# Hybrid attention layer: key and query projection moved two units ahead, MoBA gating interleaved with attention

## The reference, cut to what matters

```python
o_a = _merge_heads(_dilated_mixture(qa, ka, va)) * jax.nn.silu(ga)
o_b = _merge_heads(_moba_attention(qb, kb, vb)) * jax.nn.silu(gb)
...
k_mean = kb.astype(jnp.float32).mean(axis=3)
gate = jnp.einsum('bhsd,bhnd->bhsn', q.astype(jnp.float32), k_mean)
gate = jnp.where(past, gate, NEG_INF)
_, sel = lax.top_k(gate, topk)
```

## Time and profile before

| what | us |
|---|---|
| median of 2 runs | 2077.74 (2073.84 to 2081.64) |
| the profiled execution | 2058.25 |
| its span, on its slowest core, core 1 | 2056.6 |
| spans of the 8 cores | 2040.9 to 2056.6 |
| busy: PE, DVE, ACT, POOL | 1395.1, 1116.9, 989.0, 374.3 |

### The profile page before, as it was taken

The page is one execution under the profiler, slowest core; times in us unless marked ns, Lnnn a source line. Parts: engine busy times, 40 slices in busy tenths (PEclk is TensorE's granted clock), DMA queues, the critical chain, the costliest instruction groups (busy, mean ns, idle before and its releaser), DMA issues.

```text
span 2056.6 us, 24938 instructions; the slowest of 8 cores (2040.9 to 2056.6 us)
## 1 busy us (share of the span) xinstructions
PE 1395.1 (68%) x7432; PEld 596.8 (29%) x7432; DVE 1116.9 (54%) x2347; ACT 989.0 (48%) x1601; POOL 374.3 (18%) x269
## 2 busy tenths in 40 slices
PE   1558888878676666757551888887858576766762
PEld 0114333323242433323110423333314242422220
DVE  0005667675746464554462566766683646464475
ACT  0035657566455464644221575765636465555300
POOL 1011111111101010102454111111111110111276
PEclk9769989898979797978775898989888888896876
DMA  9362020202201000022656202022020200010233
GB/s 304 106 118 28 1 21 1 21 3 20 22 1 16 6 1 1 3 39 64 171 184 114 21 1 22 1 21 22 1 22 1 21 1 1 1 29 13 71 124 133
DMA packets 91868, 90.07 MB, mean 44 GB/s; under 512 B 69246, under 2 KB 73600, under 8 KB 91484
## 3 DMA queue, kind: packets, MB, share of 16 engines
q1 hardware_dynamic: 21020, 67.51, 10.4%
q0 software_dynamic: 70720, 20.98, 10.2%
HBM read 92.67 MB, written 16.78 MB: 53 GB/s over the span
## 4 chain that ended last, share of the span: by engine, by line
PE 45%; DVE 17%; ACT 12%; issue 11%; DMA 7%; POOL 4%; SPq 2%; DVEq 0%; ACTq 0%; POOLq 0%
PE st L578 12%; PE ot L623 11%; PE st L291 7%; PE pr L521 6%; ACT pbuf L585 5%; DMA QT<-x 4%; PE pp L536 3%; ACT pbuf L590 3%; PE pp L203 2%; POOL QT L794 2%; POOL KT L792 2%; DVE tmpf L318 2%; DVE kms L380 2%; DMA modp<-bada 2%; DVE pbuf L602 1%
## 5 line engine op out<-in xcount | busy, mean ns | idle before, releaser
L585 ACT ACTIVATE pbuf<-st 128x1024 bf16<-128x1024 f32 x384 | 381.3, 1024 | 175.6 <-PE st L578 173.6
L578 PE MATMUL st<-QT,KT 64*128 64x512 bf16 (+7 forms) x1280 | 377.7, 379 | 106.0 <-ACT pbuf L585 43.9
L623 PE MATMUL ot<-pbuf,Vt 128*128 128x512 bf16 (+3 forms) x1280 | 366.3, 370 | 68.7 <-DVE pbuf L602 50.5
L643 POOL TENSOR_TENSOR catT<-rcp,catT 64x512 bf16<-64x512 f32 x128 | 147.6, 1153 | 1139.2 <-DVE rcp L639 733.7
L602 DVE TENSOR_TENSOR pbuf<-pbuf,maskA_sb 128x512 bf16<-128x512 bf16 (+3 forms) x640 | 258.9, 451 | 174.9 <-ACT pbuf L585 125.8
L590 ACT ACTIVATE pbuf<-st 128x512 bf16<-128x512 f32 (+3 forms) x512 | 192.7, 441 | 322.0 <-PE st L578 320.0
L291 PE MATMUL st<-hT,wball 128*128 128x512 bf16 x1088 | 257.4, 383 | 68.6 <-DMA wball<-w_in 68.6
L639 DVE TENSOR_TENSOR rcp<-ot,rcp 64x512 f32<-64x512 f32 x128 | 88.1, 689 | 240.0 <-ACT rcp L637 239.7
L758 PE MATMUL st<-wball,catT 128*128 128x512 bf16 x512 | 145.7, 451 | 83.5 <-DVE KT L769 76.1
L623 PEld LDWEIGHTS ot<-pbuf,Vt 128*128 128x128 bf16 x1280 | 97.3, 100 | 281.1 <-issue 236.8
L578 PEld LDWEIGHTS st<-QT,KT 64*128 64x128 bf16 (+1 forms) x1280 | 91.6, 99 | 286.9 <-issue 257.2
(11 more groups left out here) (94 smaller groups left out, 1343.5 us busy)
## 6 DMA issues: line engine op xcount, KB each, us to landing
wball<-w_in POOLq DMA_DIRECT2D x64, 256.0 KB, 7.4
QT<-x SPq DMA_DIRECT2D x32, 512.0 KB, 4.9
y<-QT SPq DMA_DIRECT2D x32, 512.0 KB, 2.9
catT<-w_ada SPq DMA_DIRECT2D x2, 4096.0 KB, 25.3
xs<-xT SPq DMA_DIRECT2D x32, 256.0 KB, 5.8
hT<-w_ada SPq DMA_DIRECT2D x1, 4096.0 KB, 22.8
QT<-xT SPq DMA_DIRECT2D x8, 512.0 KB, 14.0
KT<-xT SPq DMA_DIRECT2D x8, 512.0 KB, 15.3
```

The costliest lines, as they stand in the source:

```text
L578: ev = op("pe", (lambda o, l, r: (lambda e: e.matmul(o, l, r, start=True, stop=True)))(stp[sti][:, jj * 512 + c0:(jj + 1) * 512], ksl[rows ...
L585: ev_e = op("act", (lambda pb_, sv, c: (lambda e: e.activation(pb_[:, :, c:512], sv[:, :, c:512], AF.Exp, scale=0.125)))(pbuf[pbi], stv, c ...
L623: ev = op("pe", (lambda o, l, r, f: (lambda e: e.matmul(o, l, r, start=f, stop=False, skip_group_check=True)))(otp[oi][:, c0:512], Vt[qi][ ...
L643: e3 = op("pool", (lambda n_, orow_, tk: (lambda e: e.tensor_tensor(catT[orow_, u, tk], n_[orow_, :], catT[orow_, u, tk], op=ALU.mult)))(r ...
```

## The change

`proj_unit` loses its gating. The loop calls it for unit u+2 after the attention of unit u, so two units are projected ahead; unit 1 is projected before the loop. The SiLU step in it works on the gate of unit u+1 (`silu_u`), and unit 7's gate, for which no projection is left, gets its SiLU alone (`silu_only`). The gating becomes a generator of 28 steps, `gating_gen`, that a new `merge3` lays beside the attention of the unit before: one attention step, one filler chunk, one gating step. It uses bank `pp` alone, and the filler uses bank `pr` alone.

```diff
@@ proj_unit
-            if u + 2 < 8:
-                load_weights(b, u + 2)
-            rope_done = S_.last("dve", "pool", "act")
...
+            state["qk_done"] = S_.last("dve", "pool", "act") + extra_ready
+            state["kmean_ev"] = kmean_ev[0]
@@ gating
-            def gating_both():
-                qts, kts = QT[qi], KT[qi]
-                gbanks = [pr, pp]
...
+        def gating_gen(b, u):
...
+                    ev = op("pe", (lambda q, h: (lambda e: e.matmul(
+                        pp[:, h * 256 + q * 16:h * 256 + (q + 1) * 16], qts[h][0:64, q * 128:(q + 1) * 128], kmhl2[0:64, h, :],
+                        start=True, stop=True)))(q16, hh),
...
+                for piece in range(4):
+                    bank = pp
+                    fkey = "pp_free"
...
+                            waits=([e11] + list(state[fkey]) if i4 == 0 else ()),
+                            sig=(True if i4 == 3 else None))
+                    yield
+                    e12 = op("dve", (lambda pc, h, bk: (lambda e: e.tensor_copy(
+                        qts[h][64:72, pc * 512:(pc + 1) * 512], bk[64:72, :])))(piece, hh, bank),
+                        waits=[ev], sig=True)
+                    state[fkey] = [e12]
+                    yield
@@ vg_filler
-            banks = [[pr[:, :], "pr_free"], [pp[:, :], "pp_free"]]
+            banks = [[pr[:, :], "pr_free"]]
...
-                bank, fkey = banks[n % 2]
+                bank, fkey = banks[0]
@@ main loop
             run(proj_unit(b, 0, hT_ready, full=True))
+            load_weights(b, 2)
+            run(proj_unit(b, 1, hT_ready, full=False, silu_u=None))
             for u in range(8):
-                ready = list(state["unit_ready"])
...
+                ready = S_.last("dve", "pool", "act") + e8_all
+                if u < 7:
+                    gg = gating_gen(b, u + 1) if u + 1 >= 4 else None
+                    merge3(att_unit(b, u, ready), vg_filler(b, u + 1), gg)
+                    state["wb_free"][(u + 1) % 2] = list(state["fill_last_pe"])
+                    if u + 3 < 8:
+                        load_weights(b, u + 3)
+                    if u + 2 < 8:
+                        run(proj_unit(b, u + 2, hT_ready, full=False, silu_u=u + 1))
+                        e8_all += e8_events()
+                    else:
...
+                        silu_only(b, u + 1)
+                else:
                     run(att_unit(b, u, ready))
-                    merge(att_unit(b, u, ready), vg_filler(b, u + 1), 1.0)
-                    run(proj_unit(b, u + 1, hT_ready, full=False))
```

More of the change, by code:

```diff
@@ L412, in proj_unit @@
                 for tt in range(4):
-                    steps += [lambda tt=tt: qk_step(1, tt), lambda tt=tt: silu_step(tt)]
+                    steps += [lambda tt=tt: qk_step(1, tt)]
+                    if silu_u is not None:
+                        steps += [lambda tt=tt: silu_step(tt)]
+                if silu_u is None:
+                    steps += [flush_step]
+                nk = len(steps)
                 steps += [lambda tt=tt: qk_step(0, tt) for tt in range(4)]
                 if is_b:
-                    steps.insert(9, flush_step)
-                    steps.insert(10, kmean_step)
+                    steps.insert(nk + 1, flush_step)
+                    steps.insert(nk + 2, kmean_step)
             pending = None
@@ L501, in proj_unit, with silu_only @@
[L501 to L504 removed]
+            state["qk_done"] = S_.last("dve", "pool", "act") + extra_ready
+            state["kmean_ev"] = kmean_ev[0]
+        def silu_only(b, u):
+            for tt in range(4):
+                tok = slice(tt * 512, (tt + 1) * 512)
+                gi = tt % 2
+                sg = rcp[gi][:, :]
+                ea = op("act", (lambda sg_, tk: (lambda e: e.activation(sg_, catT[:, u, tk], AF.Exp, scale=-1.0)))(sg, tok),
+                        waits=list(state["rc_free"][gi]) + list(state["fill_done"]), sig=True)
+                ea = op("act", (lambda sg_: (lambda e: e.activation(sg_, sg_, AF.Ln, bias=onet[:, 0:1])))(sg), waits=[ea], sig=True)
+                ea = op("act", (lambda sg_: (lambda e: e.activation(sg_, sg_, AF.Exp, scale=-1.0)))(sg), waits=[ea], sig=True)
+                ev_d = op("dve", (lambda sg_, tk: (lambda e: e.tensor_tensor(catT[:, u, tk], catT[:, u, tk], sg_, op=ALU.mult)))(sg, tok),
+                          waits=[ea], sig=True)
+                state["rc_free"][gi] = [ev_d]
@@ L660, in run, with merge3 @@
                 pass
+        def merge3(ga, gb, gc_):
+            done_b = gb is None
+            done_c = gc_ is None
+            for _ in ga:
+                if not done_b:
+                    try:
+                        next(gb)
+                    except StopIteration:
+                        done_b = True
+                if not done_c:
+                    try:
+                        next(gc_)
+                    except StopIteration:
+                        done_c = True
+            if not done_b:
+                for _ in gb:
+                    pass
+            if not done_c:
+                for _ in gc_:
+                    pass
         def merge(ga, gb, ratio):
```

144 lines of the change are left out of this document (72 added, 72 removed).

## The result

The changed kernel takes 2234.71 us (median of 11 runs, 2226.12 to 2249.12). Beside it on the same chip the kernel before takes 2066.72 us (10 runs, 2053.41 to 2092.69). The ratio is 1.084, with an interval of 1.0801 to 1.0879: **slower by 8.4%**; the two medians are 168 us apart. Forecast were +87 us and 2165 us, with a range from 2070 to 2250.

What follows compares the result with a forecast made beforehand. PE was taken to set the pace of the attentions and DVE the end of the gaps. The terms -115 + 103 + 80 + 9 + 10 gave +87 us, put onto the median 2077.74 as 2165 us, range 2070 to 2250.

Steps and rivals of the forecast that it cites:

- the forecast's own signs of being wrong: Idle time only moves and attentions keep their length; B gap does not shrink; attentions' clock falls well under 0.88 and 0.95.
- Gating leaves the gap: Gap before each of 8 B units: scores no longer wait for the gating, 14.4 us each, -115 us.
- what is moved: Unit 1's projection before the first attention and unit 7's SiLU alone: +9 us, from 0 to 15.
- The filler on one bank: In 14 fillers, a group's first chunk waits for the previous group's casts: +103 us, from 50 to 180.
- The clock: PE's granted clock falls to 0.50 at single longer waits in attentions, up to 1.7 us each: +10 us, 0 to 60.
- the second rival: PE's clock falls at each longer wait in the attentions: some +120 in place of +10, 2275 us; chance 0.12.
- The gating inside an attention: Added PE work and transposes waiting for casts in 8 host attentions: +80 us, from 36 to 144.
- The waits absorbed: Rival: new waits fall into PE's existing idle time in attentions, only work is added: -60, 2018 us; chance 0.14.
- half made good: Rival: hand-over terms in attentions shrink, +103 to 52 and 80 to 60: +10, 2088 us; chance 0.12.

Runs made afterwards that it cites:

- one bank alone: The kernel before with only the filler's second bank taken away, so every filler group uses bank pr: 2278.42 us, ratio 1.1076.
- the waits filled: The changed kernel with 38 unread matmuls per attention added before the filler's first chunks, in attentions 0 to 2 only: 2165.39 us, ratio 1.0528.
- early casts: The changed kernel with the casts of filler and gating written one attention step earlier, ahead of the next step's masks: 2009.83 us, ratio 0.9776.
- late casts of the gating: The changed kernel with the filler's casts one step earlier, but the gating's left behind the masks: 2106.08 us, ratio 1.0207.
- a second bank: The changed kernel with the filler alternating between pr and pp again in attentions 0 to 2: 2120.88 us, ratio 1.0332.
- the fastest version: The changed kernel with casts one step earlier, `ready` narrowed, key sums moved into the attention before, two filler banks in attentions 0 to 2: 1906.9 us, ratio 0.9235.

## Why the forecast had the sign right and the size at half

Of the forecast's own signs of being wrong one came: the granted clock in the attentions fell well under the 0.88 and 0.95 of before, to 0.69 to 0.77 in A units and 0.81 to 0.85 in B units. Attentions 0 to 2 are 19.8 us longer on the mean instead of some 9, unit 3's 24.4 instead of some 20, those of units 4 to 6 19.6 instead of some 15.

**Gating leaves the gap, and what is moved: right.** -111 us measured for all gaps and starts, against -115 and +9. The B gap is 34.9 us as forecast, the SiLU gap 11.1 us, the A gap unchanged, and the first scores follow DVE's last rotary instruction at once.

**The filler on one bank: right as a price of waits.** 8.7 us per A attention were forecast. Measured are 8.8 in attention 2 of the changed kernel, 7.4 with one bank alone, and 9.3 with the waits filled (56 us in six). In a B unit 5.6 were forecast, and 5.1 measured with one bank alone. Not the whole wait of a chunk is lost, as the working had it. On core 1 the chunks of attention 2 wait 13.5 us, but PE's idle time before its scores and its products into `ot` falls by 4.7, which leaves 8.8. In all the chunks wait 130 us after the change, where 180 had been expected, and the transposes 50 (40 to 100).

**The clock: the step that failed.** The term was +10 us, from 0 to 60: stretches at the lower level were to come at single places, 1.7 us each. In the six attentions 0 to 2 alone they cost 63 us, some 10 an attention and as much as the waits, and PE's busy time shows it without any experiment, +10.4 us for the same instructions in attention 2. With one bank alone it is 12.0 in an A unit and 5.1 in a B unit; over 8 and 6 of them that is an estimated 127 us. Both factors of the term were too small. All four gate groups of attention 2 came with such a stretch, and the stretches were 3.4 to 13.7 us long. The price of 3.4 came from the earlier trace rows, but the trace of before also held a long one, at the start of attention 2 (core 1), where the scores had waited 3.86 us:

```profile
372.00:388.70 16.70, 16.62 (x66) 6.08 (x66) 6.74 (x17) 7.97 (x14) 1.14 (x1) 0.50 0.51 45
388.70:439.60 50.90, 43.28 (x255) 16.20 (x254) 35.00 (x82) 36.43 (x57) 6.90 (x6) 1.00 0.00 1
```

Behind it the clock stays at 1.00, though PE waits six times for 0.9 to 1.1 us.

The argument against the second rival, that PE is busy on both sides of each wait, did not hold: the rows around 443 us show the drop in just such a place. That rival, at 2275, came nearer to the result (40 us) than the forecast at 2165 (70 us), and 0.12 was too little for it. Its own term for the clock was +120. What the attentions took (+287) over the forecast's waits and work (+183) is 104; of it 63 are shown to be clock by the filled waits, and 41, in attentions 3 to 6, were not taken apart by an experiment.

The Trainium skill's page "TensorE: Matmul & The Clock Gate", section "A second HAM failure mode: psum-queue depth-cycling", was named beside that rival. The trace agrees with it in kind: short waits between groups, clock to 0.50 and back. The section gives no price for it; the 10.4 us of 67.8 here are one.

**The gating inside an attention: near in B units, too high in unit 3.** Forecast were 9 us in a B host and 13 in unit 3, +80 in all. Beside the run with one bank alone it is 9.4 (+57 over six) and 4.5 (+9 over two), +66, and this has the lost clock in it, which the forecast had in another term. How much of that price is the place of the casts, the other runs show. With early casts unit 4's attention is 7.6 us over before, of which the filler's share isn't taken apart, and late casts of the gating add 10.0; in unit 3 it is 3.6 and 11.1. How much of the 91 us for these late casts would stay at full clock was not tried; PE's longer busy time says about half.

**The waits absorbed, half made good:** both rivals are out. In attention 2 PE's idle time was 7.6 us; now it is 16.4. That is the forecast's price in full, and nothing of it was made good.

That 2234.71 lies in the range from 2070 to 2250 is partly luck. The forecast started from a median of 2077.74, the kernel before took 2066.72 beside the result; from 2077.74 the measured ratio would give 2252 us, just above the range. As a difference +87 was forecast and +168 (medians) to +174 (profiled executions) measured, about double. The range held it only because it took in up to half of the clock's rival. The sign is settled by either.

## What to carry to other kernels

When a buffer of PSUM becomes single, look at what stands ahead of its evacuation (the copy that empties it) in the evacuating engine's stream before counting buffers: writing the casts ahead of the next step's masks instead of behind them was worth 225 us here. In attentions 0 to 2, where the two remedies can be held against each other, early casts gave 101 us and a second bank 107 to 115. Price a wait of TensorE twice, once as idle time and once as slower matmuls behind it, if rows of the kernel already show the clock falling after shorter ones. And work issued further ahead gave nothing here while its consumer still waited for the last event of every engine; narrowing that event gave 27 us, and taking DVE's sums out from ahead of it 38.

## What the runs showed of the hardware

- Waits of 2.6 to 3.3 us on PE, with PE busy on both sides, are accompanied by stretches of 3.4 to 13.7 us at a granted clock of 0.50 (attention 2 after, four such waits); the mean in an attention went from 0.88 to 0.75 or so. In attention 2 before, six waits of 0.9 to 1.1 us are followed by none.
- Adding work made the kernel faster: 38 matmuls (389 ns each on the mean) in each of six attentions, put into the waits, raised the clock to 0.88 to 0.95 and took 63 us out of these attentions.
- Full clock over a whole attention with its filler was seen only in the fastest version: on core 6 two attentions of A units of 65.4 and 64.9 us at 1.00. The shortest before on any core was 65.4 us, at 0.95.
